# A chunked RWKV-7 recurrence on one core: three elementwise products of each pair of scans move from VectorE to GpSimd

## The chip, the cores and the metric

The kernel runs on one core of a Trainium2 chip. The metric is the device time of one execution in microseconds, from the first instruction to the last; lower is better. Everything is computed in float32, except where the code marks bfloat16 constants. The engines named below are TensorE (PE, with its weight loads PEld), VectorE (DVE), ScalarE (ACT), GpSimd (POOL) and SyncE (SP), which issues most transfers. Each engine works through its own list of instructions in order and waits on semaphores for the others.

## The reference, cut to what matters

One layer with 128 context tokens and 256 latent tokens: a modulated RMSNorm, one projection `z = h @ w_in`, two token mixers on it (a bidirectional RWKV-7 scan and grouped-query attention), a gated merge, an output projection, and a top-4-of-32 mixture of experts. The change lies in the scan:

```
kk = normalised(k * rw_kk)
for d in range(2):                              # forward and backward
    w_log = -softplus(-(w0[d] + tanh(wd[d]) @ w2[d])) - 0.5
    decay = exp(-exp(w_log))
    a = sigmoid(a0[d] + ad[d] @ a2[d])
    kd = k * (1 + (a - 1) * ka)
    y, s_fin = rwkv_scan(r, decay, kd, v, kk, a, s0[d], reverse=(d == 1))
    bonus.append(sum(r * kd * r_k, over a head's 64 channels) * v)
# one step of the scan:
#   S = S * w - (S kk) (kk a)^T + v kd^T ;  y = S r
```

## The kernel before, in words

**Stages.** Four stages follow one another. First the modulation and the input projection, with attention woven into them. Then the recurrence. Then the merge, the output projection, the second norm and the router. Last a loop over expert blocks, in which 12 MB of weights for each expert stream from HBM through 18 places of 1 MB each while TensorE multiplies. The expert weights wait for the merge (`upm`, `mrg`, `wout`) before their transfers are issued, since their places are in use until then. So no expert work starts before the recurrence is over.

**The recurrence.** There are three tiles of 128 tokens (tile 0 is context, 1 and 2 are latent) and two directions. `pairs` joins a forward tile and a backward tile, index `d` being the direction: (0, 0), then (1 forward, 2 backward), then (2 forward, 1 backward). One turn of the loop `for p, pair in enumerate(pairs)` computes both scans of a pair, in chunks of 64 tokens. Each engine has the same loop, in its own order. A turn consists of:

- low-rank products on TensorE, their tanh on ScalarE, and from them on VectorE the log decay `LW`, the rate `AA`, the key `KD` and `T2 = kk * a` (L1728 to L1736);
- cumulative sums of `LW` on TensorE, and their exponentials on ScalarE: `EQ` (L1349), `EN` (L1351), `ER` (L1352) and a few columns (L1354). The semaphore `lexp` counts four of these for each direction;
- four products of 128x512 for each direction on VectorE: `RQ[d][:, 0]` (L1740), `BK[d][:, 0]` (L1742), `BK[d][:, 1]` (L1743) and `RQ[d][:, 1] = r * ER` (L1745). The last is the receptance-times-decay operand of the title;
- 32 transposes on TensorE (L725), four for each product, in that same order, each group of four waiting for its product; ScalarE copies each group out of PSUM (L1235);
- Gram products on TensorE, masked on VectorE (L1760) into `AM`, then an inversion by five levels of products, TensorE and VectorE in turn (L1777, L1781, and a 32x32 transpose L1784);
- the bonus products `BON = KD * r` (L1786) and `BON = BON * r_k` (L1787) on VectorE, two instructions each, one for each direction;
- TensorE forms `WT` and `UV`, which ScalarE copies; then two steps `k` over the chunks: `UU` on VectorE (L1795 in the very first step, where the state is zero, L1799 in all others), state and output products on TensorE, sums on VectorE (L1809 to L1834). At `k == 1` VectorE first reduces `BON` over heads (L1790).

**What shares space.** All these tiles lie in one buffer, `work`. `BON` lies on `XM`, the transposed inverse, and at the start of `BKT`; `KD` lies on `UU`. So `BON` may be written only when the last level is over, and `UU` only when `KD` has been read.

**GpSimd** has nothing to do in the recurrence: its list goes from the third `kk` normalisation (L660) to the first normalisation of the output (L664), both small powers of 128x8. The lines that fix this order are

```
for j in range(NT):
    gp.wait_ge(S["kkss"], NT + j + 1)
    gp.tensor_tensor(stat[:, 16:24], stat[:, 8:16], half[:, 0:8], rs).then_inc(S["kkr"], 1)

for j in range(NT):
    gp.wait_ge(S["kkss"], 2 * NT + j + 1)
    gp.tensor_tensor(stat[:, 16:24], stat[:, 8:16], half[:, 0:8], rs).then_inc(S["kkr"], 1)
```

## Time and profile before

| | us |
|---|---|
| median of 3 runs | 1624.02 |
| lowest and highest run | 1620.69, 1624.89 |
| span of the profiled execution | 1626.1 |
| of it, the recurrence (270 to 500 us) | 230 |
| of it, the expert blocks (from 565 us) | 1061 |

Over the span TensorE is busy 91%, VectorE 32%, ScalarE 16% and GpSimd 6%. The profiled execution's span lies 2.1 us above the median of the runs. A busy share over the span mixes stages with different limits, so the stages are read apart: the expert blocks show the 16 DMA engines busy 98% of the time, and the recurrence shows them idle (7%) with TensorE, VectorE and ScalarE handing work to each other. A row of the timeline gives the start in us, the duration in us, the engine, the line, the operation, the tiles written and read with their shape, and the count of merged instructions; in brackets stands the idle time of the engine before it and what ended it.

### The profile page before, as it was taken

Reading aid. Unit: us, or ns where it says so; the run is one execution under the profiler, and the core shown is the slowest. Engines: PE = TensorE matmul, PEld = TensorE weight load, DVE = VectorE, ACT = ScalarE, POOL = GpSimd, SP = SyncE. Lnnn points to the kernel's source line nnn. Section 1 sums busy time; section 2 is a strip of 40 time slices with the busy share of each in tenths; the row PEclk is TensorE's granted clock in tenths of the full one; section 3 lists DMA queues with packets and bytes.
Section 4 is the critical chain, followed back from the end, with each engine's and each line's share of the span. In section 5 each row is a group of like instructions: output and inputs, shape, how many; then the busy total and the mean of one; then the engine's idle time right before and its main releaser. Section 6 shows DMA issues by size and latency. Waiting matters only on the chain.

```text
span 1626.1 us, 26117 instructions
## 1 busy us (share of the span) xinstructions
PE 1471.8 (91%) x10008; PEld 709.2 (44%) x10009; DVE 524.1 (32%) x976; ACT 262.0 (16%) x514; POOL 100.1 (6%) x191
## 2 busy tenths in 40 slices
PE   4899998988997977999989999999999998998994
PEld 1677666767783452333323333333332332332331
DVE  2564544777777652101101101101011011110126
ACT  0332333221300210101101101101111010110110
POOL 1000000000001000000000000000000000000021
PEclk8899998999897977999999999999999999999996
DMA  9556835000016486999999999999999999999995
GB/s 363 201 191 238 324 133 187 2 9 3 2 55 218 148 353 278 420 421 421 422 421 421 422 421 421 422 421 422 422 420 422 421 421 421 420 422 422 421 406 189
DMA packets 97928, 510.78 MB, mean 314 GB/s; under 512 B 14752, under 2 KB 17072, under 8 KB 45160
## 3 DMA queue, kind: packets, MB, share of 16 engines
q1 hardware_dynamic: 82680, 480.08, 72.7%
q10 hardware_dynamic: 10336, 17.18, 2.8%
q0 software_dynamic: 4848, 12.59, 2.1%
q8 instruction: 50, 0.82, 0.2%
q14 instruction: 14, 0.11, 0.0%
HBM read 491.03 MB, written 22.71 MB: 316 GB/s over the span
## 4 chain that ended last, share of the span: by engine, by line
PE 64%; DMA 15%; DVE 10%; SPq 7%; issue 3%; ACT 1%; POOL 0%; DVEq 0%; ACTq 0%; POOLq 0%
PE bank L718 51%; PE bank L722 10%; SPq L595 6%; DMA ring<-w_moe_in 5%; DMA work<-w_moe_in 3%; DMA spare<-w_moe_in 3%; PE bank L725 3%; DVE work L2052 1%; DMA zbuf<-w_ada 1%; DMA work<-rows_d,dest 1%; DVE work L1781 1%; DVE work L1760 1%; DVE work L2053 1%; DVE work L1784 1%; ACT work L1235 1%
## 5 line engine op out<-in xcount | busy, mean ns | idle before, releaser
L718 PE MATMUL bank<-work 64*64 64x64 f32 (+3 forms) x5134 | 534.0, 355 | 39.0 <-DMA work<-w_moe_in 9.6
L718 PEld LDWEIGHTS bank<-work 64*64 64x64 f32 (+2 forms) x5134 | 246.4, 137 | 289.4 <-issue 235.8
L718 PE MATMUL bank<-ring,work 128*64 128x512 f32 (+1 forms) x1376 | 352.4, 606 | 17.0 <-DMA ring<-w_moe_in 10.9
L2046 DVE TENSOR_SCALAR work<-bank 128x512 f32<-128x512 f32 x39 | 27.0, 692 | 752.1 <-PE bank L718 752.1
L718 PEld LDWEIGHTS bank<-ring,work 128*64 128x64 f32 (+1 forms) x1376 | 115.4, 145 | 224.8 <-issue 192.8
L1235 ACT ACTIVATE work<-bank 128x512 f32<-128x512 f32 (+2 forms) x223 | 110.6, 513 | 561.5 <-PE bank L718 323.1
L722 PE MATMUL bank<-parts 128*128 128x512 f32 (+1 forms) x720 | 167.1, 386 | 3.0 <-DVE parts L448 3.0
L718 PE MATMUL bank<-zbuf,work 64*64 64x64 f32 (+2 forms) x966 | 139.1, 387 | 12.7 <-DMA zbuf<-w_moe_in 4.7
L722 PEld LDWEIGHTS bank<-parts 128*128 128x128 f32 x720 | 128.5, 190 | 33.6 <-issue 5.2
L1462 ACT ACTIVATE work<-work 128x512 f32<-128x512 f32 x39 | 24.6, 630 | 468.9 <-DVE work L2046 468.9
L718 PEld LDWEIGHTS bank<-zbuf,work 64*64 64x64 f32 (+2 forms) x966 | 65.2, 141 | 76.3 <-issue 58.5
L725 PE MATMUL bank<-ident,work 128*128 128x128 f32 (+1 forms) x340 | 67.1, 315 | 22.1 <-DVE work L2053 11.3
L448 DVE TENSOR_TENSOR parts<-ring,parts 128x1024 fp32r<-128x1024 f32 (+1 forms) x40 | 45.7, 1145 | 75.9 <-ACT parts L443 75.9
L725 PEld LDWEIGHTS bank<-ident,work 128*128 128x128 f32 (+1 forms) x340 | 47.5, 177 | 49.4 <-DVE work L2053 32.5
L718 PE MATMUL bank<-spare,work 128*64 128x512 f32 (+1 forms) x256 | 62.0, 563 | 3.2 <-ACT work L1235 2.2
L683 POOL TENSOR_TENSOR half<-half 128x1 f32<-128x1 f32 x38 | 7.0, 185 | 844.0 <-PE bank L725 831.1
L718 PE MATMUL bank<-first,work 128*64 128x512 f32 x208 | 53.0, 611 | 1.9 <-DMA first<-w_moe_in 1.9
L443 ACT ACTIVATE parts<-ring 128x1024 fp32r<-128x1024 f32 (+1 forms) x40 | 39.6, 994 | 76.7 <-PE bank L722 72.7
L2052 DVE TENSOR_SCALAR work<-bank 128x256 f32<-128x256 f32 x78 | 32.9, 421 | 55.3 <-PE bank L718 55.3
L670 POOL DMA_INDIRECT zbuf<-h_d,slots x39 | 41.0, 1052 | 19.8 <-issue 19.8
L718 PE MATMUL bank<-rowc 96*64 96x512 bf16 x234 | 39.9, 392 | 1.8 <-issue 1.8
L725 PEld LDWEIGHTS bank<-ident,zbuf 128*128 128x128 f32 x204 | 24.5, 153 | 37.8 <-issue 37.7
(264 smaller groups left out, 862.6 us busy)
## 6 DMA issues: line engine op xcount, KB each, us to landing
work<-w_moe_in SPq DMA_DIRECT2D x108, 1024.0 KB, 22.8
ring<-w_moe_in SPq DMA_DIRECT2D x84, 1024.0 KB, 25.6
work<-w_moe_out SPq DMA_DIRECT2D x64, 1024.0 KB
ring<-w_moe_out SPq DMA_DIRECT2D x44, 1024.0 KB, 22.1
ring<-w_ada SPq DMA_DIRECT2D x11, 2048.0 KB, 7.7
zbuf<-w_moe_in SPq DMA_DIRECT2D x22, 1024.0 KB, 26.7
first<-w_moe_in SPq DMA_DIRECT2D x21, 1024.0 KB
spare<-w_moe_in SPq DMA_DIRECT2D x21, 1024.0 KB
```

What stands on the lines that cost most here:

```text
L443: nc.scalar.activation(zpart(t, 0, n), z_quarter(t), ACT.Copy).then_inc(S["hi"], 1)
L448: eng.tensor_tensor(zpart(t, 1, n), z_quarter(t), zpart(t, 0, n), ALU.subtract)\
L595: sp.dma_start(place_of(turn_e, c), src).then_inc(s_place[(WC * turn_e + c) % NPLACE], 16)
L670: gp.indirect_dma_start(xg, None, h2_d.rearrange("t (h n) -> (t h) n", h=2), bass.IndirectOffsetOnAxis(ap=slots[:, 0:1], axis=0), bounds_c ...
L718: return pe.matmul(out, l, r, start=start, stop=stop)
L722: return pe.matmul(out, l, r, start=start, stop=stop, skip_group_check=True)
L725: return pe.transpose(out, src, ident[0:n, 0:n])
L1235: cp = lambda out, src, scale=1.0: sc.activation(out, src, ACT.Copy, scale=scale)
L1462: sc.activation(th, gl, ACT.Tanh, scale=ALPHA / 2).then_inc(S["thd"], 1)
L1760: tt(dst, bk(d, 2 * par + i).rearrange("p (c n) -> p c n", c=2), gramm[:, d:d + 1, :].broadcast_to([P, 2, 4 * HC]), M).then_inc(S["am"], 1)
L2046: ts(gl, B[0], LIMIT, None, ALU.min).then_inc(S["thd"], 1)
L2052: LL(ts(uu[:, seg], B[1][:, seg], LIMIT, -LIMIT, ALU.min, ALU.max))
```

## The change

VectorE no longer forms `RQ[d][:, 1]`, nor the two products of `BON`. GpSimd does, in the same loop over `pairs`, on the same tiles. Its loop stands between the two groups of small powers. For each pair it issues `RQ[0][:, 1]`, `RQ[1][:, 1]`, each after its own `ER`; then `KD * r` for both directions, each after the last level of that direction; then both multiplications by `r_k`. That is six instructions of 128x512 for a pair, 18 in all.

Two new semaphores say when they are done. `rq1` counts the `RQ[d][:, 1]`, and TensorE waits for it before the fourth group of transposes of a direction. `bonq` counts the four bonus products of a pair. VectorE waits for two of them before it writes `UU`, because `UU` lies on `KD`, and for all four before it reduces `BON`. Three semaphores go for it: `tcA` and `tcV` become one, `tcs`, and `lnld` is counted on `stld`, with the same waits in effect.

```
+            for p, pair in enumerate(pairs):
+                for d, j in pair:
+                    gp.wait_ge(S["lexp"], 4 * (2 * p + d) + 3)
+                    gp.tensor_tensor(RQ[d][:, 1, :], zbuf[:, j, ZR:ZR + DR], ER[d], ALU.mult).then_inc(S["rq1"], 1)
+                for d, j in pair:
+                    gp.wait_ge(s_d[d], NP * p + LEVELS - 1)
+                    gp.wait_ge(s_x[d], NX * p + NX)
+                    gp.tensor_tensor(BON[d], KD[d], zbuf[:, j, ZR:ZR + DR], ALU.mult).then_inc(S["bonq"], 1)
+                for d, j in pair:
+                    gp.wait_ge(S["bonq"], 4 * p + d + 1)
+                    gp.tensor_tensor(BON[d], BON[d], rkb, ALU.mult).then_inc(S["bonq"], 1)
...
-                    for i, (key, need, src, b) in enumerate((("rqd", 1, RQ[d][:, 0, :], 1), ("bkd", 1, BK[d][:, 0, :], 3),
-                                                             ("bkd", 2, BK[d][:, 1, :], 0), ("rqd", 2, RQ[d][:, 1, :], 2))):
-                        pe.wait_ge(S[key], 2 * u + need)
+                    for i, (key, need, src, b) in enumerate((("rqd", u + 1, RQ[d][:, 0, :], 1), ("bkd", 2 * u + 1, BK[d][:, 0, :], 3),
+                                                             ("bkd", 2 * u + 2, BK[d][:, 1, :], 0), ("rq1", u + 1, RQ[d][:, 1, :], 2))):
+                        pe.wait_ge(S[key], need)
...
                     tt(BK[d][:, 1, :], KD[d], EN[d], M).then_inc(S["bkd"], 1)
-                    ve.wait_ge(S["lexp"], 4 * u + 3)
-                    tt(RQ[d][:, 1, :], zr[d], ER[d], M).then_inc(S["rqd"], 1)
...
-                both(*[tt(BON[d], KD[d], zr[d], M) for d in range(2)])
-                both(*[tt(BON[d], BON[d], rkb, M) for d in range(2)])
                 for k in range(2):
                     if k == 1:
+                        ve.wait_ge(S["bonq"], 4 * p + 4)
                         both(*[ve.tensor_reduce(bonus[:, j, d, :], hv(BON[d]), X, A_) for d, j in pair])
                     for d, j in pair:
                         r = rows_of(chunk_of(k, d))
                         ve.wait_ge(s_uc[d], 4 * p + 4)
+                        ve.wait_ge(S["bonq"], 4 * p + 2)
```

On VectorE, from the end of `T2` to the first Gram mask of the first pair, the list before reads (L1745 is `RQ[d][:, 1]`, L1752 a small product of 128x4, L1760 the masks):

```order
L1736 TENSOR_TENSOR work<-ky,work 128x512 x2
L1740 TENSOR_TENSOR work<-ky,work 128x512
L1742 TENSOR_TENSOR work<-work 128x512
L1743 TENSOR_TENSOR work<-work 128x512
L1745 TENSOR_TENSOR work<-zbuf,work 128x512
L1740 TENSOR_TENSOR work<-ky,work 128x512
L1742 TENSOR_TENSOR work<-work 128x512
L1743 TENSOR_TENSOR work<-work 128x512
L1745 TENSOR_TENSOR work<-zbuf,work 128x512
L1752 TENSOR_TENSOR smallc<-smallc 128x4 x2
```

and in the changed kernel, where lines lie 7 to 9 further down:

```order
L1745 TENSOR_TENSOR work<-ky,work 128x512 x2
L1749 TENSOR_TENSOR work<-ky,work 128x512
L1751 TENSOR_TENSOR work<-work 128x512
L1752 TENSOR_TENSOR work<-work 128x512
L1749 TENSOR_TENSOR work<-ky,work 128x512
L1751 TENSOR_TENSOR work<-work 128x512
L1752 TENSOR_TENSOR work<-work 128x512
L1759 TENSOR_TENSOR smallc<-smallc 128x4 x2
```

Eight products have become six; nothing else in this stretch has moved. On VectorE after the last level of the first pair, the list before reads (L1781 the last subtraction, L1795 `UU`):

```order
L1781 TENSOR_TENSOR work<-work,bank2 128x512
L1781 TENSOR_TENSOR work<-work,bank6 128x512
L1786 TENSOR_TENSOR work<-work,zbuf 128x512 x2
L1787 TENSOR_TENSOR work<-work,rowc 128x512 x2
L1795 TENSOR_SCALAR work<-work 64x512 x2
L1814 TENSOR_TENSOR work<-bank0,smallc 128x256
```

and in the changed kernel:

```order
L1788 TENSOR_TENSOR work<-work,bank2 128x512
L1788 TENSOR_TENSOR work<-work,bank6 128x512
L1802 TENSOR_SCALAR work<-work 64x512 x2
L1821 TENSOR_TENSOR work<-bank0,smallc 128x256
L1821 TENSOR_TENSOR work<-bank4,smallc 128x256
L1841 COPY ky<-bank1 64x512
```

The four bonus products are gone, and `UU` follows the last subtraction at once. On GpSimd the 18 products now stand between the small powers (L659 and L674 here):

```order
L659 TENSOR_TENSOR stat<-stat,half 128x8 x3
L664 TENSOR_TENSOR work<-zbuf,work 128x512 x2
L668 TENSOR_TENSOR work<-work,zbuf 128x512 x2
L671 TENSOR_TENSOR work<-work,rowc 128x512 x2
L664 TENSOR_TENSOR work<-zbuf,work 128x512 x2
L668 TENSOR_TENSOR work<-work,zbuf 128x512 x2
L671 TENSOR_TENSOR work<-work,rowc 128x512 x2
L664 TENSOR_TENSOR work<-zbuf,work 128x512 x2
L668 TENSOR_TENSOR work<-work,zbuf 128x512 x2
L671 TENSOR_TENSOR work<-work,rowc 128x512 x2
L674 TENSOR_TENSOR stat<-stat,half 128x8 x3
```

Where the list before went from L660 straight to L664, nothing stood between. The lists of TensorE, ScalarE and SyncE hold the same instructions in the same order as before; only waits have other names and counts.

## Rows read from the trace of the kernel before

**Rows 1.** Stages: us, busy us (count) of each engine, PEclk, DMA share, GB/s.
```profile
270.00:500.00 230.00, 202.66 (x4183) 167.48 (x4184) 167.31 (x292) 51.07 (x105) 0.00 (x0) 0.93 0.07 22
...
565.00:1626.00 1061.00, 973.33 (x4499) 348.43 (x4497) 179.20 (x372) 119.43 (x251) 77.55 (x172) 0.96 0.98 404
```

**Rows 2.** The chain that ended last, by engine, whole span.
```profile
PE 64%; DMA 15%; DVE 10%; SPq 7%; issue 3%; ACT 1%; POOL 0%; DVEq 0%; ACTq 0%; POOLq 0%
```

**Rows 3.** The same chain in time order, first pair: start us, us, what.
```profile
292.13 1.08 PE bank L718 x32
...
293.31 4.89 DVE work L1760 x8
...
298.24 11.26 PE bank L718 x144
```

**Rows 4.** Timeline of VectorE, first pair, around the four products.
```profile
285.19 1.29 DVE L1736 TENSOR_TENSOR work<-ky,work 128x512 f32<-128x512 f32 x2
286.52 0.69 DVE L1740 TENSOR_TENSOR work<-ky,work 128x512 f32<-128x512 f32 x1
...
290.74 0.69 DVE L1745 TENSOR_TENSOR work<-zbuf,work 128x512 f32<-128x512 f32 x1
```

**Rows 5.** Timeline of ScalarE, first pair: the two ER.
```profile
284.82 0.59 ACT L1352 ACTIVATE work<-bank 128x512 f32<-128x512 f32 x1
...
287.43 0.59 ACT L1352 ACTIVATE work<-bank 128x512 f32<-128x512 f32 x1
```

**Rows 6.** Timeline of TensorE: the 32 transposes of each pair.
```profile
287.54 4.59 PE L725 MATMUL bank<-ident,work 128*128 128x128 f32 x32
...
364.54 3.69 PE L725 MATMUL bank<-ident,work 128*128 128x128 f32 x32
...
437.64 3.82 PE L725 MATMUL bank<-ident,work 128*128 128x128 f32 x32
```

**Rows 7.** Timeline of VectorE: first product of the second and third pair.
```profile
361.81 0.69 DVE L1740 TENSOR_TENSOR work<-ky,work 128x512 f32<-128x512 f32 x1
...
435.84 0.69 DVE L1740 TENSOR_TENSOR work<-ky,work 128x512 f32<-128x512 f32 x1
```

**Rows 8.** Groups on GpSimd, whole span: busy us, mean ns, idle before.
```profile
L683 POOL TENSOR_TENSOR half<-half 128x1 f32<-128x1 f32 x38 | 7.0, 185 | 844.0 <-PE bank L725 831.1 <-ACT lists L1434 12.9
...
L648 POOL MEMSET spare<- 128x1024 f32 x1 | 1.0, 952 | 0.3 <-POOLq L2122 0.3
...
L649 POOL MEMSET half<- 128x16 f32 x1 | 0.1, 115 | 0.0
```

**Rows 9.** Timelines of VectorE and GpSimd where both ran together, twice.
```profile
227.23 1.22 DVE L448 TENSOR_TENSOR parts<-ring,parts 128x1024 fp32r<-128x1024 f32 x1
...
227.40 2.54 POOL L660 TENSOR_TENSOR stat<-stat,half 128x8 f32<-128x8 f32 x1 [26.03 <-DVE stat L1646]
...
501.89 1.64 POOL L664 TENSOR_TENSOR stat<-stat,half 128x8 f32<-128x8 f32 x1 [271.95 <-DVE stat L1850]
...
501.92 0.72 DVE L1852 TENSOR_TENSOR states<-zbuf,stat 128x512 f32<-128x512 f32 x1
...
503.63 0.69 DVE L1854 TENSOR_TENSOR work<-work,stat 128x512 f32<-128x512 f32 x1 [0.99 <-POOL stat L664]
```

**Rows 10.** Timelines around the bonus products, first pair; last row second pair.
```profile
329.26 0.69 DVE L1781 TENSOR_TENSOR work<-work,bank 128x512 f32<-128x512 f32 x1 [0.24 <-PE bank L718]
330.27 0.69 DVE L1781 TENSOR_TENSOR work<-work,bank 128x512 f32<-128x512 f32 x1 [0.32 <-PE bank L718]
...
332.20 1.29 DVE L1787 TENSOR_TENSOR work<-work,rowc 128x512 f32<-128x512 f32 x2
333.53 0.87 DVE L1795 TENSOR_SCALAR work<-work 64x512 f32<-64x512 f32 x2
...
331.77 1.15 ACT L1235 ACTIVATE work<-bank 128x512 f32<-128x512 f32 x3 [0.26 <-PE bank L718]
333.17 0.60 ACT L1235 ACTIVATE work<-bank 128x512 f32<-128x512 f32 x1 [0.25 <-PE bank L718]
...
334.00 0.34 PE L718 MATMUL bank<-work 64*64 64x64 f32 x4 [0.87 <-DVE work L1795]
...
407.49 1.55 DVE L1799 SCALAR_TENSOR_TENSOR work<-bank,work 64x256 f32<-64x256 f32 x4 [1.34 <-PE bank L718]
```

More of the change, by code:

```diff
@@ L351, in build @@
         names = """adald cond modld n1 xld modd ssq rstd htok htr hTa hTv wdone zmm zA zV cons2 cons3
[L352 to L354 removed]
+        cachekv stored aqk kdupd qtr ktr qTa kTv smm nmax prob rinv ptr ptc pv ya tg ttr tcs kkss kkr stld sttr stev lora lt1 ltanh lw lcum lexp rqd bkd ttr4 rqT wsm s0p gram am yout
+        yrd twod st2 sftr sfcp sfout gld gps yfin ytr yTc upm upad mga mrg mtr mTc wout g1l x1s
         h2out h2tr h2Tc lg tabled summed sqd b32 b3d cmpd idxm idxc xgd xtm xtc gmm mult hi thd actd atm atc
[L356 removed]
+        yc yo fin chain uud rsc gpn zfill chain2v rq1 bonq modrow condq routeq""".split()
         S = {n: sem("s_" + n) for n in names}
```

15 lines of the change are left out of this document (5 added, 10 removed).

## The prediction

> **What bounds the kernel now.** I read the stages first, then the chain that ended last, then the timeline of the three places that the change touches. The stages [rows 1] show two different kernels. In the expert blocks the transfers are busy 98% of 1061 us, so only the weight stream counts there, and the change touches none of it. That stream starts when the merge is done, so whatever the recurrence gains or loses shifts the rest of the span one for one. In the recurrence, 230 us, the transfers are idle and TensorE is busy 202.66 us; the whole chain is 64% TensorE and 10% VectorE [rows 2]. It is a hand-over between engines: after the transposes the Gram products, then eight masks on VectorE, then TensorE again, with 0.1 us between them [rows 3]. Nothing there has slack, so a delay of the last transpose arrives at the end of the span in full. What VectorE computes is worth time only where its result comes later than TensorE is ready for it. That is asked place by place.
>
> **The receptance-times-decay product, before.** In the first pair the eight products run from 286.52 to 290.74 + 0.69 = 291.43 [rows 4], one every (290.74 - 286.52) / 7 = 0.60 us, and the 32 transposes end at 287.54 + 4.59 = 292.13 [rows 6], 0.70 us after the last product. TensorE alone needs 3.69 us, as the second pair shows [rows 6], 0.46 us for each of eight groups. So in the first pair it is held up by VectorE for 0.9 us. In the second pair the products start at 361.81 [rows 7] and end at about 366.7, while TensorE runs to 368.23 at its own pace: no hold. In the third they start at 435.84 and end at about 440.75; the transposes take 3.82 us, held by 0.13.
>
> **Taking two of eight products away** leaves VectorE with five steps of 0.60 and the last of 0.69, 3.69 us from the first start. If nothing else changed, the first pair's last product would end at 290.21, and two groups of transposes would still follow it, 0.70 + 0.46 = 1.16 us: 291.37 instead of 292.13, a gain of 0.75. The third pair gains its 0.13, the second nothing. This is all that the first half of the change can gain, 0.9 us.
>
> **What a product costs on GpSimd.** No row shows GpSimd multiplying 512 columns. A multiplication of one column takes 0.19 us, and one stream into SBUF costs (952 - 115) / (1024 - 16) = 0.83 ns a column [rows 8], 0.43 us for 512 columns. With one stream at a time of the three that a product has (two read, one written), a product lasts 0.19 + 3 x 0.43 = 1.46 us; with all three at once 0.62. I take two reads in turn with the write half hidden, 1.25 us, of which 1.06 is moving data and 0.19 fixed. The page "GPSIMD Engine Reference" of the Trainium skill, section "Performance versus the Vector engine", gives 2.6 cycles a column at 1.2 GHz for a two-input float32 operation; from it my estimate would be 1.1 us and the fixed part, which agrees, but no run here shows it.
>
> **Is 1.25 us early enough?** `ER` of the first pair is there at 285.41 and 288.02 [rows 5]. GpSimd would be done by about 286.7 and 289.3, before TensorE reaches groups 4 and 8. Time alone is no problem, unless the two engines are in each other's way.
>
> **Are they?** Twice the trace has GpSimd start beside a VectorE instruction that reads two tensors from SBUF. At 227.40 a power of 128x8 began 0.17 us into such an instruction of 1.22 us and took 2.54 us instead of the 1.64 of its like: 0.90 late, about until the VectorE instruction was through its columns [rows 9]. At 501.89 the power came first, and VectorE's product of 128x512, started 0.03 later, took 0.72 instead of 0.69 [rows 9], though the power ran until 503.53. I read this as: while one of them reads for two, the other's reads wait; but GpSimd holds this path only as long as it moves data, a moment for 8 columns, and not through its arithmetic. For 512 columns it moves data nearly all the time, so I let it hold VectorE for 1.06 us each. The Trainium skill, "SBUF — State Buffer", section "Who interferes with whom", says that a VectorE instruction with two SBUF inputs and a GpSimd instruction that reads SBUF exclude each other, the first to come holding on for its whole instruction. The rows agree on the exclusion and contradict the whole instruction, since 0.72 us fitted inside the 1.64. With the whole duration of 1.25 the sum below would be 4.7 instead of 3.6.
>
> **The first sum.** `ER` arrives while VectorE is in its run of two-input products (L1736 runs from 285.19, [rows 4, 5]), so both GpSimd products fall into that run and push it by 2 x 1.06 = 2.12 us. Last VectorE product: 286.52 + 3.69 + 2.12 = 292.33; last transpose 1.16 later, 293.49, against 292.13: +1.4. Second pair: 361.81 + 3.69 + 2.12 + 1.16 = 368.78 against 368.23: +0.55. Third: 435.84 + 6.97 = 442.81 against 441.46: +1.35. Together +3.3 us. With a hold of 0.43 each it would be +0.2, with 1.27 it would be +4.6.
>
> **The bonus products.** In the second pair `UU` waits 1.34 us for TensorE after them [rows 10], so on VectorE they cost nothing, and taking them away gains nothing; the third pair looks alike. On GpSimd the two that `UU` now waits for are done about 2.5 us after the last level, which is before TensorE is. Only in the first pair, where the state is zero, did TensorE wait for VectorE: 0.87 us at 334.00, behind the bonus products [rows 10]. There `UV` of the forward scan is copied by 332.4 and that of the backward one by 333.77, so `UU` could be up to 0.87 us earlier. But the first subtraction ends at 329.95, so GpSimd's first two products end at 331.2 and 332.5, and its third, a multiplication by `r_k`, starts at once and reads until 333.7. `UU` (L1795) takes 0.43 us for 512 columns where products take 0.69, a fast form that I expect to exclude GpSimd as well: 333.75 instead of 333.53. I count +0.3, between -0.87 (no exclusion) and +1.3 (its second half behind the fourth product also). The reduction comes 8 us later and waits for nothing. The merged semaphores cost nothing: each wait still ends with the same event.
>
> **The sum.** +3.3 and +0.3 are +3.6 us on a span of 1626.1. Since the median of the runs is 2.1 below the span, I put the same difference on it: 1624.0 + 3.6 = 1627.6. A measurement of this kernel can tell about 0.3%, 4.9 us, from no change, so this would be read as the same.
>
> **Rivals.** *No contention that matters* (chance 0.32). If GpSimd and VectorE share the path column by column, or GpSimd slips into gaps, VectorE's run is shorter by two products and `UU` comes early: -0.75 - 0.13 - 0.87 = -1.75 us, 1622.3. For it speaks the 0.72 us; against it the 0.90 us of delay at 227.40. *GpSimd is starved* (0.17). VectorE's products follow each other with no gap, the next beginning 0.09 us before the last one ends. If GpSimd gets its turn only when that run is over, the first `RQ[0][:, 1]` starts at 290.25 and is ready at 291.5; then five groups of transposes follow, 4 x 0.46 + 0.70 = 2.54: 294.05, +1.9. Second pair: run over at 365.5, 366.75, 369.3, +1.1. Third: 439.55, 440.8, 443.35, +1.9. With +0.3 for `UU`, +5.2: 1629.2. This is the mechanism on the slower side. It is decided by who is served at the border between two VectorE products, and passes 4.9 us once a GpSimd product lasts over 1.15 us. For it speaks that the power at 227.40 started late by the rest of the VectorE instruction; that row doesn't show a second one behind it with two inputs. *GpSimd's price is above 1.46 us* (0.04), since no large product is in the trace: then each 0.25 us more costs six holds, 1.5 us, on top of the +4.6: some 1631. My own case holds 0.47. That the change would not move the work is no case: the lists of instructions show it moved.
>
> **Numbers.** Chances: mine 0.47, no contention 0.32, starved 0.17, dearer 0.04. From the ends of the price, mine reaches from about 1624 to 1629.5; the runs of the kernel before spread from 1620.7 to 1624.9. To hold 8 in 10 the range takes in the no-contention case and the starved one: 1621 to 1631. Slower by over 0.3%: a quarter of mine, half of the starved, the dearer, 0.24. Faster by over 0.3% needs -4.9 us where at most -1.75 is to be had, so only the spread could give it: 0.05. The same: 0.71.
>
> **What would show it.** On GpSimd 18 products of 128x512, of about 1.25 us or longer where they wait. On VectorE one product in three of the run at the four-product place lasting or starting about 1 us late; if all six follow at 0.60, there is no contention. The transposes of the pairs: 293.5, 368.8 and 442.8 less their starts in my case, and a wait for `RQ[d][:, 1]` before group 4 in the starved case. `UU` of the first pair at 333.75 shows contention, at 332.6 none. The prediction is wrong if the gap between engines elsewhere in the recurrence changes, for instance by the granted clock, 0.93 in this stage [rows 1].

## The result, and the profile after

| | before | changed |
|---|---|---|
| first comparison, median of four runs each, us | 1622.8 | 1637.5 |
| lowest and highest of them | 1620.7, 1624.9 | 1634.9, 1641.1 |
| ratio, 95% interval | | 1.0093 [1.0071, 1.0115] |
| second comparison (e8 below), ratio, interval | | 1.0041 [1.0012, 1.0070] |
| mean of every run measured | 1624.7 (109 runs) | 1634.8 (15 runs) |

The changed kernel is slower, by 14.7 us in the first comparison and by 10.1 us (0.6%, give or take some 3 us) over all runs. Two executions in a slower state, one of the kernel before at 5714.7 us and one of e6 at 2475.3, are left out of every number here. The prediction was +3.6 us, 1627.6, with a range from 1621 to 1631: the sign was right, the size was not, and the time lies above the range. The experiments below are read against 1624.7 for before and 1634.8 for the change; a ratio compares each kernel with runs of before on the same chip.

The profiled execution of the changed kernel has a span of 1636.2 us and its run took 1638.2. The stages answer to [rows 1]: us, then busy us and count of TensorE, its weight loads, VectorE, ScalarE and GpSimd, then the granted clock, the DMA share and GB/s.

```profile
270.00:500.00 230.00, 201.17 (x4138) 165.80 (x4139) 160.69 (x266) 52.02 (x105) 23.83 (x18) 0.93 0.07 22
...
565.00:1626.00 1061.00, 979.46 (x4522) 352.46 (x4520) 180.60 (x369) 119.76 (x248) 73.78 (x169) 0.96 0.98 405
```

VectorE has 6.6 us less to do in the recurrence and GpSimd 23.8 us more. The expert blocks stay bound by the weight stream. They are the same length in both traces (1626.1 - 622.52 = 1003.6 from their first product to the end before, 1636.2 - 632.57 = 1003.6 after), so the loss lies ahead of them and is passed on one for one, as predicted. Of the 10.1 us between the two spans 7.9 lie in the recurrence. Another 2.6 lie between the recurrence and the expert blocks, where the change touches nothing: that part takes 124.0 us in this trace of before and 126.6 in that of the change, but 119.3 to 126.6 over all 18 traces and 126.4 in another run of before. So a pair of traces measures the change only inside the recurrence. By engine the last chain reads as in [rows 2], with TensorE three points down, VectorE and SyncE's queue one up:

```profile
PE 61%; DMA 15%; DVE 11%; SPq 8%; issue 3%; ACT 1%; POOL 0%; DVEq 0%; ACTq 0%; POOLq 0%
```

GpSimd holds 0% of it. That is the trap of this view: GpSimd is on the path nowhere, it only makes the engine that is on the path slower. The three groups of products on GpSimd (busy us, mean ns of one, idle before):

```profile
L664 POOL TENSOR_TENSOR work<-zbuf,work 128x512 f32<-128x512 f32 x6 | 8.8, 1463 | 114.2 <-ACT smallc L1363 114.2
...
L671 POOL TENSOR_TENSOR work<-work,rowc 128x512 f32<-128x512 f32 x6 | 7.7, 1299 | 0.0
...
L668 POOL TENSOR_TENSOR work<-work,zbuf 128x512 f32<-128x512 f32 x6 | 7.5, 1274 | 119.1 <-DVE work L1788 119.1
```

L664 is `RQ[d][:, 1]`, L668 `KD * r`, L671 the multiplication by `r_k`. Where VectorE is quiet one takes 1.25 us (L668 in the first pair: 2.51 for two, below), the price that the prediction had estimated from small rows.

**Where the time goes.** I set marks by the first TensorE product of each part, in us from the start of the first pair's low-rank products. "Low-rank to Gram" holds what the first half of the change touches, and summed over three pairs it is one number per trace; "Gram 1 to pair 2" holds the inversion, the bonus products and the scan of the first pair.

| trace | low-rank to Gram, pairs 1, 2, 3 | sum | Gram 1 to pair 2 | whole recurrence |
|---|---|---|---|---|
| before | 16.1, 16.9, 15.8 | 48.8 | 59.2 | 222.6 |
| before, another run (e16) | 15.9, 15.9, 14.7 | 46.5 | 62.5 | 222.1 |
| changed | 19.1, 17.3, 17.3 | 53.6 | 64.1 | 230.5 |
| changed (e8) | 18.4, 17.2, 17.6 | 53.2 | 63.3 | 230.4 |
| changed (e14) | 19.0, 16.0, 16.0 | 51.0 | 59.8 | 224.5 |

Two things stand out. The first column of sums separates the kernels. The second does not: both have a short form of it, near 59.5, and a long one, 62.5 to 64. The whole recurrence takes 228.5 us in the mean of the three traces of the change and 222.3 in the two of before, some 6 us more. So part of the 14.7 us belongs to the change and part to which form a run draws.

### The first pair, read closely

VectorE, for [rows 4] (start us, us, engine, line, operation, tiles, count, and in brackets the idle time before and what ended it):

```profile
284.73 2.37 DVE L1745 TENSOR_TENSOR work<-ky,work 128x512 f32<-128x512 f32 x2
287.13 0.69 DVE L1749 TENSOR_TENSOR work<-ky,work 128x512 f32<-128x512 f32 x1
287.74 1.76 DVE L1751 TENSOR_TENSOR work<-work 128x512 f32<-128x512 f32 x1
289.42 0.68 DVE L1752 TENSOR_TENSOR work<-work 128x512 f32<-128x512 f32 x1
...
291.22 0.68 DVE L1752 TENSOR_TENSOR work<-work 128x512 f32<-128x512 f32 x1
```

GpSimd in the same stretch:

```profile
285.03 1.52 POOL L664 TENSOR_TENSOR work<-zbuf,work 128x512 f32<-128x512 f32 x1 [54.42 <-ACT smallc L1363]
287.64 1.31 POOL L664 TENSOR_TENSOR work<-zbuf,work 128x512 f32<-128x512 f32 x1 [1.09 <-ACT smallc L1363]
```

The two `T2` products (L1745) take 2.37 where [rows 4] has 1.29, a hold of 1.08. The product at 287.74 takes 1.76 instead of 0.69, a hold of 1.07, exactly beside the second GpSimd product. Two holds, and the other products at their usual step of 0.60. GpSimd's own two take 1.52 and 1.31 instead of 1.25: I read the 0.27 and 0.06 as its wait for the VectorE instruction under way. In the second and third pair the holds are 0.95 to 1.07 and GpSimd's extra 0.10 to 0.38. So the engines take turns at the border of an instruction, and the one that waits is served next; GpSimd was not starved. VectorE's run ends at 291.90. The prediction had 292.33, and this trace runs 0.46 earlier at the pair's start (275.50 against 275.96), which makes 291.87. This step was right to 0.03 us. (Two holds of 1.08 and 1.07 are 2.15 where it had 2.12.)

TensorE, for [rows 6]:

```profile
287.97 0.63 PE L735 MATMUL bank<-ident,work 128*128 128x128 f32 x4 [0.74 <-DVE work L1749]
289.55 5.11 PE L735 MATMUL bank<-ident,work 128*128 128x128 f32 x28 [0.96 <-DVE work L1751]
294.59 1.65 PE L728 MATMUL bank<-work 64*64 64x128 f32 x52
```

Here the prediction went wrong. It let the last transpose end 1.16 us after the last VectorE product; it ended 2.76 after it (294.66 - 291.90). The holds fell at groups 1 and 2, where TensorE had nothing in hand, so it stood 0.74 and 0.96 us. Those stops alone would have been made good: the products that follow come every 0.60 us and a group takes 0.46. But then it did 28 transposes in 5.11 us, where the rate of the second pair before [rows 6] gives 28 x 3.69 / 32 = 3.2. Record by record, they start every 0.109 us at first; from 290.44 to 293.64 fifteen of them start every 0.213 us, 1.6 us more than at the first rate; then it is 0.109 again. That is the whole of 2.76 - 1.16 = 1.60. The granted clock tells why. First the changed kernel, then the kernel before, from 290 to 300 us (columns as in the stages):

```profile
290.00:300.00 10.00, 9.46 (x186) 8.76 (x184) 6.32 (x13) 4.49 (x8) 0.00 (x0) 0.83 0.01 2
```

```profile
290.00:300.00 10.00, 8.70 (x210) 7.36 (x209) 8.29 (x16) 3.86 (x7) 0.00 (x0) 1.00 0.01 3
```

After the two stops part of this stretch ran at 1.2 GHz, with 0.83 as the mean; before, all of it ran at 2.4 GHz. TensorE is busier (9.46 against 8.70 us) and gets less done (186 instructions against 210). For TensorE alone from 290 to 294 us the changed kernel reads

```profile
290.00:294.00 4.00, 4.00 (x22) 0.57 0.00 0
```

and the kernel before 88 instructions at 1.00. This fall is no accident of one run. In 2 us pieces the granted clock comes down to between 0.50 and 0.60 at this place in all six traces in which GpSimd's reads make TensorE stop for 0.74 and 0.96 us (three of the change, e1, e3, e7). It is 1.00 from 286 to 300 us in the other twelve, among them e5 below, whose stops of 0.40 and 0.67 us are made by VectorE alone. What of it brings the fall, the length of the stops or something else that these six share, no run separates.

In the second and third pair no clock fell behind the holds, and there the prediction's step held. In the third:

```profile
442.61 2.19 PE L735 MATMUL bank<-ident,work 128*128 128x128 f32 x16
445.48 2.21 PE L735 MATMUL bank<-ident,work 128*128 128x128 f32 x16 [0.68 <-DVE work L1749]
447.61 1.65 PE L728 MATMUL bank<-work 64*64 64x128 f32 x52
```

TensorE waits once, 0.68 us, between the directions, where [rows 6] has 32 transposes without a break. VectorE's last product ends at 446.54, and the last transpose 1.15 us later (442.61 to 447.69 in all); in the second pair it is 1.16. From the start of `RQ[0][:, 0]` to the last transpose it takes 6.89 and 6.88 us in these pairs, for the predicted 6.97, and 6.42 and 5.62 before. So by the rows the three pairs lose 3.0, 0.5 and 1.3 us, 4.7 in all for the predicted 3.3, and the 1.6 us of low clock are more than the whole difference.

### The bonus products and UU, first pair

GpSimd, then VectorE, then TensorE, for [rows 10]:

```profile
332.63 2.51 POOL L668 TENSOR_TENSOR work<-work,zbuf 128x512 f32<-128x512 f32 x2 [43.68 <-DVE work L1788]
335.09 2.68 POOL L671 TENSOR_TENSOR work<-work,rowc 128x512 f32<-128x512 f32 x2
```

```profile
331.79 0.69 DVE L1788 TENSOR_TENSOR work<-work,bank 128x512 f32<-128x512 f32 x1 [0.24 <-PE bank L728]
332.80 0.69 DVE L1788 TENSOR_TENSOR work<-work,bank 128x512 f32<-128x512 f32 x1 [0.32 <-PE bank L728]
335.24 2.82 DVE L1802 TENSOR_SCALAR work<-work 64x512 f32<-64x512 f32 x2 [1.75 <-POOL work L668]
```

```profile
336.69 0.34 PE L728 MATMUL bank<-work 64*64 64x64 f32 x4 [0.74 <-DVE work L1802]
...
338.11 0.46 PE L728 MATMUL bank<-work 64*64 64x64 f32 x4 [0.22 <-DVE work L1802]
```

`UU` waits 1.75 us for GpSimd's `KD * r`, and then its two halves take 2.82 us instead of the 0.87 of [rows 10]: each is held by one of the two `r_k` products, 0.98 us. TensorE gets the first half 4.21 us after the end of the first subtraction (336.69 - 332.48), where before it was 334.00 - 329.95 = 4.05: +0.16 for the predicted +0.3. But the second half arrives late too, and TensorE stops a second time for it, 0.22 us. The products of that row take 0.46 instead of 0.34: the clock is lower again.

### The profile page after: what moved, and what is told of

Same layout as the page of the kernel before. It is cut to its first block, busy times and chain, and to the rows that moved or that the text cites. A ratio compares the mean times of both kernels' runs of the same rounds, so it can differ in the third digit from the quotient of the medians.

```text
span 1636.2 us, 26126 instructions
## 1 busy us (share of the span) xinstructions
PE 1474.5 (90%) x10008; PEld 713.5 (44%) x10009; DVE 521.3 (32%) x958; ACT 262.9 (16%) x514; POOL 123.7 (8%) x209
## 4 chain that ended last, share of the span: by engine, by line
PE 61%; DMA 15%; DVE 11%; SPq 8%; issue 3%; ACT 1%; POOL 0%; DVEq 0%; ACTq 0%; POOLq 0%
PE bank L728 49%; PE bank L732 10%; SPq L594 8%; DMA ring<-w_moe_in 5%; DMA spare<-w_moe_in 3%; DMA work<-w_moe_in 3%; PE bank L735 3%; DMA zbuf<-w_ada 1%; DVE work L2059 1%; DMA work<-rows_d,dest 1%; DVE work L1788 1%; DVE work L1767 1%; DVE work L2060 1%; DVE work L1791 1%; ACT work L1244 1%
## 5 line engine op out<-in xcount | busy, mean ns | idle before, releaser
L735 PE MATMUL bank<-ident,work 128*128 128x128 f32 (+1 forms) x340 | 70.4, 326 | 25.6 <-DVE work L2060 11.5
```

The costliest lines, as they stand in the source:

```text
L735: return pe.transpose(out, src, ident[0:n, 0:n])
```

## The experiments

The times and marks of all of them but e14 to e16, which are one traced run each. A mean stands beside its difference from 1624.7. The means of before differ by up to 2 us from one set of runs to another (1623.8 to 1625.8), so the ratio, taken on the same chip, is the surer number. e6 is the same kernel as e12.

| kernel | ratio to before, 95% | mean us, against before | low-rank to Gram, sum | Gram 1 to pair 2 | recurrence |
|---|---|---|---|---|---|
| e1 only `RQ[:, 1]` | 1.0048 [1.0028, 1.0068] | 1632.1, +7.4 | 53.7 | 59.8 | 227.5 |
| e2 only bonus | 1.0018 [0.9991, 1.0044] | 1627.3, +2.6 | 47.3 | 63.6 | 223.8 |
| e3 products added | 1.0058 [1.0041, 1.0076] | 1633.1, +8.4 | 53.2 | 59.8 | 226.9 |
| e4 memsets added | 0.9983 [0.9965, 1.0001] | 1625.1, +0.4 | 49.1 | 59.0 | 222.9 |
| e5 VectorE longer | 1.0029 [1.0009, 1.0050] | 1629.9, +5.2 | 52.6 | 62.5 | 229.7 |
| e7 change, `r_k` behind `UU` | 1.0010 [0.9992, 1.0029] | 1628.3, +3.6 | 52.0 | 59.3 | 223.2 |
| e8 change again | 1.0041 [1.0012, 1.0070] | 1634.2, +9.5 | 53.2 | 63.3 | 230.4 |
| e9 e2, `r_k` behind `UU` | 0.9985 [0.9969, 1.0001] | 1621.5, -3.2 | 46.4 | 58.5 | 217.2 |
| e10 VectorE, `r_k` behind `UU` | 1.0000 [0.9980, 1.0020] | 1624.2, -0.5 | 46.5 | 58.5 | 217.5 |
| e6 and reductions earlier | 0.9939 [0.9916, 0.9963] | 1619.3, -5.4 | 46.6 | 58.3 | 216.7 |
| e12 the same again | 0.9968 [0.9953, 0.9984] | 1619.7, -5.0 | 46.6 | 57.4 | 216.6 |
| e11 `UU` split | 1.0013 [0.9996, 1.0029] | 1626.3, +1.6 | 47.7 | 59.5 | 220.2 |
| e13 `UU` split wider | 1.0021 [0.9997, 1.0044] | 1627.1, +2.4 | 47.0 | 64.7 | 224.4 |

### Which half costs what: e1 and e2

e1 keeps the first half of the change and puts the bonus products back on VectorE:

```
-                    gp.tensor_tensor(BON[d], KD[d], zbuf[:, j, ZR:ZR + DR], ALU.mult).then_inc(S["bonq"], 1)
...
-                    gp.tensor_tensor(BON[d], BON[d], rkb, ALU.mult).then_inc(S["bonq"], 1)
...
+                both(*[tt(BON[d], KD[d], zr[d], M) for d in range(2)])
+                both(*[tt(BON[d], BON[d], rkb, M) for d in range(2)])
```

> Only the receptance-times-decay products are on GpSimd, the bonus products stay on VectorE. In the changed kernel's trace the transposes came 2.98, 1.38 and 1.52 us later, relative to the stage around them, 5.9 us in all, and the rest of the 10.1 us between the two spans lay in stretches with a lower granted TensorE clock. Exclusion theory (VectorE is held 1.08 us by each of the six products, and only that costs): +5 to +7 us, about 1629. Clock theory (TensorE's stall in the first pair makes the granted clock fall later, and that is the larger part): +10 to +15 us, as the whole change. Bonus theory (the bonus half is the costly one, by the late UU and the slow stretch from 338 us): under +5 us.

e2 keeps the bonus half and puts the other back:

```
-                    gp.tensor_tensor(RQ[d][:, 1, :], zbuf[:, j, ZR:ZR + DR], ER[d], ALU.mult).then_inc(S["rq1"], 1)
...
+                    ve.wait_ge(S["lexp"], 4 * u + 3)
+                    tt(RQ[d][:, 1, :], zr[d], ER[d], M).then_inc(S["rqd"], 1)
```

> Only the bonus products are on GpSimd, all eight products of the run stay on VectorE. Exclusion theory: only the first pair's UU is late, +0.2 to +0.5 us at the first, so the time stays within 1 us. Bonus theory: the second half of UU is held by the second r_k product, TensorE waits 0.74 and then 0.22 us, the granted clock is 0.58 from 338 to 350 us as in the changed kernel, and the time is +5 us or more.

Measured: +7.4 and +2.6, together +10.0, the whole change +10.1. Within the noise the halves add up, so there is no sign that one hides the other. Most of the loss is in the first; the second alone is not clear of no change (its interval begins at 0.9991).

The marks say the same. Eleven traces without GpSimd products or longer VectorE work at the first place (before twice, e2 twice, e4, e6, e9 to e13) have sums of 46.4 to 49.1, mean 47.3. Five with them (the change three times, e1, e7) have 51.0 to 53.7, mean 52.7. The two sets don't overlap, and by these means the first half costs 5.4 us there (4.7 by the rows above), where 3.3 was predicted. The first pair alone takes 18.4 to 19.1 instead of 15.7 to 16.1: nearly 3 us for the predicted 1.4.

### Contention or missing work: e3 and e4

e3 takes nothing from VectorE and adds six GpSimd products whose result nobody reads, at the time of `ER` (it and e4 also count `lnld` on `stld`, as the change does, and VectorE waits for the added work before `UU`):

```
+            spot = first[:, 1536:2048]
...
+                for d, j in pair:
+                    gp.wait_ge(S["lexp"], 4 * (2 * p + d) + 3)
...
+                    gp.tensor_tensor(spot, zbuf[:, j, ZR:ZR + DR], rkb, ALU.mult).then_inc(S["rq1"], 1)
```

> The kernel before with all its products on VectorE, and six products of 128x512 more on GpSimd whose result nobody uses, issued when each ER is ready, as in the change. Exclusion theory: two VectorE products of each run are held 1.08 us each, 8 products plus 2.16 us, transposes of the three pairs later by about 2.1, 1.2 and 2.0 us: +5 us directly, more than the receptance half of the change since no product is taken away. If what costs is the dependence of TensorE on GpSimd's result and not the shared path: 0 us.

e4 puts two writes without reads in the place of each product:

```
+                    gp.wait_ge(S["lexp"], 4 * (2 * p + d) + 3)
+                    for n in range(2):
...
+                        gp.memset(spot, 0.0).then_inc(S["rq1"], 1)
```

> As the run with the extra products, but GpSimd writes 512 columns of zeros twice at each of the six places and reads nothing from SBUF. If it is GpSimd's reads that exclude VectorE's second input: all eight products of the run keep 0.60 us from start to start and the time is that of before, within 0.2%. If any GpSimd work beside VectorE holds it, or GpSimd's activity lowers TensorE's clock: +0.3% or more, as with the extra products.

Measured: +8.4 us and +0.4 us. VectorE and GpSimd of e3, same place:

```profile
283.63 2.36 DVE L1743 TENSOR_TENSOR work<-ky,work 128x512 f32<-128x512 f32 x2
...
286.64 1.76 DVE L1749 TENSOR_TENSOR work<-work 128x512 f32<-128x512 f32 x1
```

```profile
283.93 1.52 POOL L668 TENSOR_TENSOR first<-zbuf,rowc 128x512 f32<-128x512 f32 x1 [54.93 <-ACT smallc L1361]
286.54 1.31 POOL L668 TENSOR_TENSOR first<-zbuf,rowc 128x512 f32<-128x512 f32 x1 [1.09 <-ACT smallc L1361]
```

And of e4:

```profile
285.44 1.29 DVE L1744 TENSOR_TENSOR work<-ky,work 128x512 f32<-128x512 f32 x2
286.76 0.69 DVE L1748 TENSOR_TENSOR work<-ky,work 128x512 f32<-128x512 f32 x1
```

```profile
285.71 1.11 POOL L669 MEMSET first<- 128x512 f32 x2 [55.43 <-ACT work L1360]
```

In e3 the same instructions as in the change take 2.36 and 1.76, though no operand has moved and TensorE waits for nothing of GpSimd's. In e4 GpSimd is busy for 1.11 us beside VectorE's two-input products, and these take their 1.29 and 0.69. So the hold is made by GpSimd's reads, not by its being busy, its semaphores or its writes. The Trainium skill, "SBUF — State Buffer", section "Who interferes with whom", says that a VectorE instruction with two SBUF inputs contends with a GpSimd instruction that reads and not with one that only writes; both traces agree. With the two products taken away from VectorE as well (e1) the time is +7.4 instead of +8.4, a difference within the noise.

### A delay without GpSimd: e5

Two unused VectorE products in each run, and nothing on GpSimd:

```
+                    if d == 0:
+                        L(tt(spot, zr[d], rkb, M))
                     tt(RQ[d][:, 0, :], kk_[d], EQ[d], M).then_inc(S["rqd"], 1)
...
                     tt(BK[d][:, 0, :], T2[d], EN[d], M).then_inc(S["bkd"], 1)
+                    if d == 0:
+                        L(tt(spot, zr[d], rkb, M))
```

> The kernel before with nothing on GpSimd; two unused products of 128x512 are added to VectorE's run of each pair, one ahead of the forward RQ, one behind the forward BK. The run is 1.2 us longer. Without any effect on the clock: transposes later by 1.2 + about 0.6 + 1.2 us, +3 us. Clock theory (any stall of TensorE there costs clock later): +8 us or more, with more slices of granted clock under 0.9 in the recurrence than before.

Measured: +5.2 us, and 52.6 at the first place, as with GpSimd. So products that come late cost about as much when VectorE alone makes them late. Its trace also has the long form of the next stretch, 62.5, which no GpSimd instruction can have made.

### The r_k products beside UU: e7, e9 and e8

e7 is the whole change with one more wait, which keeps the `r_k` products behind both halves of the first `UU`. e9 is e2 with the same line. e8 is the whole change once more, beside e7.

```
+                gp.wait_ge(S["uud"], n_step(p, 0, 1))
                 for d, j in pair:
                     gp.wait_ge(S["bonq"], 4 * p + d + 1)
                     gp.tensor_tensor(BON[d], BON[d], rkb, ALU.mult).then_inc(S["bonq"], 1)
```

> The changed kernel, but GpSimd starts the two multiplications by r_k of a pair only when both UU of its first step are written, so they can't meet UU. Exclusion theory: UU of the first pair takes 0.87 us again instead of 2.82 and starts when the first two bonus products are done; TensorE is later than before by at most 0.2 us there instead of 0.2 and another 0.2. If that double stall is what lowers the clock behind it: the stretch from 338 us is at full clock and the kernel is 3 to 5 us faster than the changed one, +0.5% on before. If the stall isn't the cause: within 1 us of the changed kernel.

> The changed kernel once more, with more runs and a second trace. Its halves alone gave +0.48% and +0.18%. If the halves add up: +0.6 to +0.7%. If they strengthen each other (both stalls in the first pair): +0.9% or more, as the first four runs said. Clock theory: again a stretch with granted clock near 0.58 right behind the late UU of the first pair, and 64 us instead of 59 from the first pair's Gram products to the second pair's low-rank products.

> Only the bonus products on GpSimd, the r_k products after UU of the first step, all eight products of the run on VectorE. With the r_k products ahead of UU this was +0.18% and showed the slow stretch from 336 us. Exclusion and clock theory: UU in two pieces of 0.42 us, TensorE waits less than before, no slow stretch behind it: -0.1 to -0.3%. If GpSimd work in the recurrence costs in itself: +0.2% again.

Measured: +3.6, +9.5 and -3.2. GpSimd and VectorE of e7:

```profile
330.42 2.51 POOL L668 TENSOR_TENSOR work<-work,zbuf 128x512 f32<-128x512 f32 x2 [43.33 <-DVE work L1789]
334.62 2.49 POOL L672 TENSOR_TENSOR work<-work,rowc 128x512 f32<-128x512 f32 x2 [1.69 <-DVE work L1803]
```

```profile
333.03 0.42 DVE L1803 TENSOR_SCALAR work<-work 64x512 f32<-64x512 f32 x1 [1.75 <-POOL work L668]
334.11 0.42 DVE L1803 TENSOR_SCALAR work<-work 64x512 f32<-64x512 f32 x1 [0.66 <-ACT work L1245]
```

The wait of 1.75 us for `KD * r` has stayed, but each half of `UU` takes 0.42 again. The `r_k` products took about 1 us from each half, and undoing that gave back 5.9 us of mean time in the change (e8 to e7) and 5.8 in its bonus half (e2 to e9); by the ratios it is 0.31% and 0.33%, 5.0 and 5.4 us, with intervals that overlap in each comparison alone. So much does not fit into two holds of 1 us, of which TensorE saw 0.2 to 0.7. The marks show where the rest is: "Gram 1 to pair 2" is 59.3 and 58.5 in e7 and e9, but 63.3 to 64.1 in two of three traces of the change and 63.6 in e2 (63.4 in e15, the same kernel). And with GpSimd in a quiet place the move costs nothing that can be measured: e9 is at 0.9985, and e10 below, the same order with everything on VectorE, at 1.0000. The window from 340 to 350 us, the change and then before:

```profile
340.00:350.00 10.00, 9.84 (x159) 9.70 (x159) 4.59 (x9) 0.00 (x0) 0.00 (x0) 0.58 0.01 2
```

```profile
340.00:350.00 10.00, 7.15 (x176) 6.90 (x172) 7.42 (x17) 0.06 (x1) 0.00 (x0) 1.00 0.01 2
```

With a granted clock of 0.58, most of ten microseconds ran at 1.2 GHz, TensorE busy throughout. That is the long form: a stretch at the low clock in the first scan, which makes some 3 to 5 us.

### What brings the low clock in the scan: e11, e13 and three more traces

If two stops of TensorE between the `UU` halves bring it, VectorE alone should be able to. e11 and e13 put a short copy before the first half of the first pair's `UU`, and one product, or a copy and two products, between the halves, all on VectorE:

```
                         if not started(p, k):
+                            L(tt(spot, zr[d], rkb, M) if d else cp(spot[:, 0:8], zr[d][:, 0:8]))
                             ts(UU[d][r], UV[d][r], -1.0, None, M).then_inc(S["uud"], 1)
```

and in e13 instead of the added line:

```
+                            L(cp(spot[:, 0:8], zr[d][:, 0:8]))
+                            for _ in range(2 * d):
+                                L(tt(spot, zr[d], rkb, M))
```

> No GpSimd. The kernel before with one unused VectorE product of 0.69 us between the two halves of each UU whose state is zero (first pair only), and a copy of 8 columns ahead of the first half. TensorE waits about 1.0 us for the first half and then again for the second, as in the changed kernel, +0.5 us directly. If stalls of TensorE there are what lowers the clock behind them, whoever causes them: granted clock clearly under that of before between 330 and 360 us (0.89 on average there, 0.75 in the changed kernel), 63 us instead of 59 to the second pair, +0.2 to +0.3%. If it takes GpSimd for that: +0.03%.

> As the run with the split UU, but with two unused VectorE products between the halves instead of one (and a copy of 8 columns ahead of each half), no GpSimd. UU's second half comes 1.4 us behind the first, as in the changed kernel, where TensorE waited a second time; directly +0.8 to +1.0 us. If a second stall of TensorE is what lengthens the slow stretch, whoever causes it: 63 us instead of 59 to the second pair's low-rank products and +0.3%. If it takes GpSimd: under +0.1%.

In e11 TensorE waited only once (1.08 us), and the stretch kept its short form, 59.5. In e13 the second stop was there:

```profile
334.55 0.34 PE L718 MATMUL bank<-work 64*64 64x64 f32 x4 [1.08 <-DVE work L1799]
...
336.54 0.34 PE L718 MATMUL bank<-work 64*64 64x64 f32 x4 [0.80 <-DVE work L1799]
...
337.06 0.52 PE L718 MATMUL bank<-work 64*64 64x64 f32 x4
```

and so was the long form, 64.7, with 0.64 of clock from 340 to 350 us:

```profile
340.00:350.00 10.00, 10.00 (x187) 9.96 (x187) 5.47 (x12) 0.00 (x0) 0.00 (x0) 0.64 0.01 2
```

Yet by mean time e13 lost only 2.4 us, and the interval takes in no change. One more trace each of the change (e14), of its bonus half (e15) and of the kernel before (e16) asked whether the form goes with the kernel.

> A third trace of the changed kernel. If the longer slow stretch in the first pair is the rule: 63 to 64 us from the Gram products of the first pair to the low-rank products of the second, as in both traces so far (64.1 and 63.3). If it was a draw: 59 to 60.

> A second trace of the bonus half. The rule: 63 to 64 us in the same stretch (63.6 in its first trace). A draw: 59 to 60.

> A second trace of the kernel before. The rule: 59.2 us in the same stretch, as in its first trace. A draw: 63.

It does not. The change, in e14, drew the short form (59.8), with its clock at 1.00 in the same window, and its run took 1629.6. The kernel before, in e16, drew the long one (62.5) with nothing changed. First e14, then e16:

```profile
340.00:350.00 10.00, 8.80 (x228) 8.66 (x227) 6.69 (x15) 0.00 (x0) 0.00 (x0) 1.00 0.01 3
```

```profile
340.00:350.00 10.00, 8.10 (x128) 7.91 (x128) 5.54 (x13) 0.00 (x0) 0.00 (x0) 0.61 0.01 2
```

So the long form is a draw. Counting traces, it came in 2 of 3 of the change, 2 of 2 of its bonus half, 1 of 2 of before, in e5 and in e13; and in none of the five with the `r_k` products behind `UU` (e6, e7, e9, e10, e12), nor in e11. That the `r_k` products beside `UU` raise its odds is what the pattern and the mean times suggest; with one or a few traces of each it isn't shown. Where the low clock begins says more. In e8, e5 and e16 it begins 8 us or more behind `UU`. It begins within 2 us of the second half of `UU` in four traces, the change, e2, e15 and e13, all of the six in which TensorE stopped a second time there (the other two are e8 and e14), and in none of the twelve without that stop. That counting was done after the traces were seen, and four of six is no rule. The run times of the change fit a draw: in e8 four of ten are 1626.4 to 1630.4 and five are 1636.7 to 1643.5.

### A better place for the bonus work: e6, e10 and e12

With GpSimd out, the remaining question is whether VectorE can do the same products at a better time. e10 moves only the `r_k` products behind the first `UU`. e6 and e12 (one kernel, measured twice) also move the reductions, from ahead of the second step's `UU` to the first step. The first of the two added pieces stands behind `UU`, the second, which e10 lacks, ahead of the output sums:

```
                 both(*[tt(BON[d], KD[d], zr[d], M) for d in range(2)])
-                both(*[tt(BON[d], BON[d], rkb, M) for d in range(2)])
                 for k in range(2):
-                    if k == 1:
-                        both(*[ve.tensor_reduce(bonus[:, j, d, :], hv(BON[d]), X, A_) for d, j in pair])
...
+                    if k == 0:
+                        both(*[tt(BON[d], BON[d], rkb, M) for d in range(2)])
...
+                    if k == 0:
+                        both(*[ve.tensor_reduce(bonus[:, j, d, :], hv(BON[d]), X, A_) for d, j in pair])
```

> No GpSimd. Everything stays on VectorE, but the multiplications by r_k come behind UU of the first step instead of ahead of it, and the two reductions of the bonus come ahead of the first step's output sums instead of ahead of the second step's UU. From the trace of before: TensorE waits 0.87 us less for UU in the first pair and 1.2 us less for UU of the second step in each pair (it waited 1.21 us behind the reductions), against output sums that are later by what of 2.6 us does not fit into gaps of 0.8, 1.3 and 1.0 us. Expected -3 us, -1 at least if the sums come late, and more if less idle time of TensorE saves clock.

> Half of the faster version: the r_k products come behind UU of the first step, the reductions stay where they were before. Directly this can give only the 0.87 us by which TensorE waited for UU in the first pair, less what of 1.3 us doesn't fit into the 0.83 us gap behind UU: -0.05% at most. If the reductions are what gave the gain: within 0.1% of before. If UU in the first pair matters beyond its wait, by the clock: -0.2% or more.

> The faster version once more, since its first measurement rested on few runs: r_k products behind the first UU, reductions ahead of the first step's output sums, all on VectorE. If -0.61% holds: between -0.4% and -0.8%, below every mean so far. If the first runs were a lucky draw of the clock: -0.2%, the 3 us that the waits alone gave.

Measured: e6 0.9939 [0.9916, 0.9963], e12 0.9968 [0.9953, 0.9984] with more runs, a mean of 1619.7, -5.0 us: faster than both kernels. e10 is at 1.0000, so the `r_k` products alone bring nothing measurable and the reductions carry the gain (1624.2 to 1619.7 us in mean, measured side by side). VectorE and TensorE at the second step of the kernel before:

```profile
340.15 1.28 DVE L1790 TENSOR_REDUCE bonus<-work 128x8 f32<-128x512 f32 x2
341.46 1.55 DVE L1799 SCALAR_TENSOR_TENSOR work<-bank,work 64x256 f32<-64x256 f32 x4
```

```profile
342.28 0.34 PE L718 MATMUL bank<-work 64*64 64x64 f32 x4 [1.21 <-DVE work L1799]
```

and of e12:

```profile
335.78 1.28 DVE L1819 TENSOR_REDUCE bonus<-work 128x8 f32<-128x512 f32 x2 [0.15 <-DVE work L1813]
...
338.95 1.55 DVE L1796 SCALAR_TENSOR_TENSOR work<-bank,work 64x256 f32<-64x256 f32 x4 [0.31 <-PE bank L718]
```

```profile
339.77 0.34 PE L718 MATMUL bank<-work 64*64 64x64 f32 x4 [0.17 <-DVE work L1796]
```

The reductions, 1.28 us, stood in front of `UU` while TensorE had nothing else: it waited 1.21 us. At 335.78 VectorE does them where before it stood idle for 1.26 and 1.00 us between copies. TensorE now waits 0.17. I had looked at the reductions as work that "waits for nothing" and not as work that something waits behind.

## Why the prediction was wrong, point by point

- **What bounds the kernel**: right. The recurrence passes its delay on one for one, the expert blocks are 1003.6 us in both traces.
- **The price of a GpSimd product**, 1.25 us: right, 1.25 (2.51 for two) alone and 1.31 to 1.63 beside VectorE. That it came out to the hundredth is luck: the estimate stood between 0.62 and 1.46.
- **The hold**, 1.06 us for each of the six products: right. It is 1.08 and 1.07 in the first pair, 0.95 to 1.07 in the others, and the end of VectorE's run was met to 0.03 us. The rivals on this point fall: "no contention" and "GpSimd is starved" are both excluded by the first pair's rows, and a price above 1.46 us by the 1.25. (The sum for a hold of 1.27 is +4.5 by the prediction's own rule, not +4.6.)
- **From the last product to the last transpose**, "1.16 later": the step that failed, in the first pair. It supposed that TensorE goes through the last groups at 2.4 GHz, 0.46 us for each. Behind its two stops fifteen transposes ran at 1.2 GHz, and the step took 2.76 us. The term of the first pair was 1.4 and measured 3.0 (294.66 - 292.13 + 0.46); without the 1.6 us of low clock it would have been right. The whole first half was 3.3 and measured 4.7 by the rows, 5.4 by the marks.
- **Second and third pair**, +0.55 and +1.35: right, +0.5 and +1.3 by the rows, with the last transpose 1.16 and 1.15 behind the last product. By the marks single traces scatter (e14 against e16 gives +0.1 and +1.3), as the clock of what stands before differs.
- **UU of the first pair**, +0.3: the first half came 0.16 later, close. The second half was named only as an upper bound of +1.3 and was the case that came: both halves held, and a second stop of TensorE.
- **The granted clock** had no term in the sum, only a last sentence as a proviso. That is the part missed: 1.2 to 1.6 us at the first pair's transposes in the three traces of the change, and 3 to 5 us in the scan behind `UU`, in two of three traces of the change. Over 104 runs of before, a run's time falls with its mean granted clock, 0.95 us for each 0.001 (correlation -0.76). The means are 0.9516 for before and 0.9486 for the change, 0.0030 lower, which is 2.8 of the 10.1 us by that slope and takes in the 1.6.
- **The ledger**: the transposes by rows and `UU` make some 5 us, the recurrence by the mean of the few traces some 6, the run times 10.1 give or take 3. What lies between 6 and 10 us is not placed.
- **The offset of the median**, -2.1: wrong in sign. A run's time is about 2 us above its span (1638.2 and 1636.2), so the span of 1626.1 should belong to a run of about 1628.1, above the runs shown. It does not touch the +3.6.
- **The range**: I took the spread of before from three runs, 4.2 us. Over 109 runs it is 1618.7 to 1633.9, with a standard deviation of 3.5. The first comparison's +14.7 had some 4.6 us of bad luck in it. But the mean of the change, 1634.8, is above the range too, so the range failed by the missing terms first.

**Open**: why the clock falls behind the two stops of the first pair's transposes, and what sets the odds of the long low-clock stretch in the scan. Two stops of TensorE between the `UU` halves precede it in the change, in its bonus half and in e13, but it also came without the second one (e16), and failed to come with it (e14); one trace says little about the mean of ten runs.

## What to carry to other kernels

An idle GpSimd is not free help beside VectorE: if it reads SBUF while VectorE is in a run of instructions with two SBUF inputs, each 128x512 product moved costs VectorE about 1.07 us where the product itself cost it 0.60 to 0.69. Where VectorE stands idle the move cost nothing that could be measured (e9), so the place decides and not the engine's own idle time. Before moving work to another engine, look for a hole in the same engine's list: here the reductions moved from ahead of `UU` into one, and the kernel gained 5 us. Where TensorE hands over every few microseconds, ask whether the work behind a new stop still gets the full clock, give that a term in the sum, and take the spread from more than three runs.

## What was not expected of the hardware

- The two engines alternate: GpSimd's products took 0.06 to 0.38 us longer only, until VectorE's instruction under way was through, though VectorE's next two-input product was already waiting.
- A one-input `TENSOR_SCALAR` of 64x512 is held too, as the prediction had guessed without a row: 2.82 us for two beside two GpSimd products, 0.42 each without (e7).
- Behind two stops of 0.74 and 0.96 us, 12 to 15 of TensorE's next transposes started every 0.213 us instead of every 0.109, in all six traces with these stops. The work behind the stops could have made them good; so the step to the last transpose took 2.35 to 2.76 us in the three traces of the change, for the 1.16 predicted.
- One and the same program draws the granted clock of a given stretch anew in each run: from 340 to 350 us it was 1.00 and 0.61 in two runs of the kernel before, 0.58 and 1.00 in two of the change, and a stretch at the low clock made some 3 to 5 us.
